# A fused transformer layer with 32 experts: slot 10 of the expert weights split into high and low words in single passes too

## The reference, cut to what matters

```python
logits = xt @ w_router + b_router            # 1024 tokens, 32 experts
top_vals, top_idx = lax.top_k(logits, 4)
gates = jax.nn.softmax(top_vals, axis=-1)
...
h = xblk @ w1[e] + b1[e]                     # w1[e] is 1024 x 2048
yb = clamped_swiglu(h) @ w2[e] + b2[e]       # w2[e] is 1024 x 1024
out = zeros.at[tok_buf].add(yb * gate_buf)   # added back by token
```

## Time and profile before

| | us |
|---|---|
| median of 3 runs | 2165.43 |
| lowest and highest | 2163.07 and 2165.44 |
| the profiled execution | 2162.8 |
| its span | 2161.1 |
| PE busy | 2080.2 (96%) |
| DVE busy | 1477.3 (68%) |
| ACT busy | 1192.9 (55%) |
| the loop of passes | 503.7 to 2147 |

### The profile page before, as it was taken

One profiled execution on the slowest core, in us unless ns is written; L12 is line 12 of the kernel. 1 busy time (PEld: TensorE's weight loads), 2 busy tenths in 40 slices (PEclk: granted clock), 3 DMA queues, 4 the chain that ended last, 5 costly groups with the idle time before them and its releaser, 6 DMA issues.

```text
span 2161.1 us, 35581 instructions
## 1 busy us (share of the span) xinstructions
PE 2080.2 (96%) x11530; PEld 1681.5 (78%) x11531; DVE 1477.3 (68%) x2291; ACT 1192.9 (55%) x1651; POOL 212.2 (10%) x201
## 2 busy tenths in 40 slices
PE   6999989988999999999999999999999999999997
PEld 4443678866799778877979797977779979888895
DVE  3251486668866787688676767678986666567666
ACT  3241375246645676567564646477764555555545
POOL 2000300012101111011010101011010110101001
PEclk9999999989999999999999999999999999999999
DMA  7000302118966699689686868679996677668556
GB/s 269 1 0 6 144 27 88 40 55 321 357 227 207 231 340 355 194 324 358 232 275 240 268 234 262 231 258 368 336 373 212 194 242 273 185 206 297 188 197 219
DMA packets 203128, 477.39 MB, mean 221 GB/s; under 512 B 14743, under 2 KB 20951, under 8 KB 203024
## 3 DMA queue, kind: packets, MB, share of 16 engines
q1 hardware_dynamic: 185598, 437.69, 55.9%
q0 software_dynamic: 17424, 39.17, 7.5%
q10 hardware_dynamic: 66, 0.02, 0.0%
HBM read 468.99 MB, written 32.11 MB: 232 GB/s over the span
## 4 chain that ended last, share of the span: by engine, by line
PE 71%; DVE 10%; issue 7%; DMA 6%; ACT 4%; DVEq 1%; ACTq 1%; POOLq 1%; SPq 0%; POOL 0%
PE ps L1288 16%; PE ps L1290 16%; PE ps L1289 16%; PE ps L1023 8%; DVE w_lo L1842 4%; DMA out<-y,idx_cur 4%; PE ps L1401 2%; DMA ring<-in_w 1%; PE ps L1168 1%; PE ps L1170 1%; PE ps L1169 1%; PE ps L1282 1%; ACT ring L719 1%; DMA xh<-in_x 1%; DVE xT L1842 1%
## 5 line engine op out<-in xcount | busy, mean ns | idle before, releaser
L890 ACT ACTIVATE w_hi<-ring 128x1024 fp32r<-128x1024 f32 x730 | 781.7, 1121 | 422.1 <-PE ps L1290 370.0
L1842 DVE TENSOR_TENSOR w_lo<-ring,w_hi 128x1024 fp32r<-128x1024 f32 x732 | 862.3, 1220 | 188.3 <-ACT w_hi L890 188.3
L1288 PE MATMUL ps<-xT,w_hi 128*128 128x256 f32 x1248 | 354.2, 284 | 0.0
L1290 PE MATMUL ps<-xT,w_lo 128*128 128x256 f32 x1248 | 353.1, 283 | 0.0
L1289 PE MATMUL ps<-xT,w_hi 128*128 128x256 f32 x1248 | 353.1, 283 | 0.0
L1288 PE MATMUL ps<-w_hi,xT 128*128 128x512 f32 x816 | 323.3, 396 | 13.2 <-issue 6.9
L1289 PE MATMUL ps<-w_lo,xT 128*128 128x512 f32 x816 | 319.5, 392 | 0.0
L1290 PE MATMUL ps<-w_hi,xT 128*128 128x512 f32 x816 | 319.5, 391 | 0.0
L1288 PE MATMUL ps<-w_hi,actT 128*128 128x512 f32 x644 | 262.8, 408 | 0.0
L1290 PE MATMUL ps<-w_hi,actT 128*128 128x512 f32 x644 | 251.6, 391 | 0.0
L1289 PE MATMUL ps<-w_lo,actT 128*128 128x512 f32 x644 | 251.1, 390 | 0.0
(11 more groups left out here) (312 smaller groups left out, 2400.7 us busy)
## 6 DMA issues: line engine op xcount, KB each, us to landing
ring<-in_w SPq DMA_DIRECT2D x390, 1024.0 KB, 7.2
xh<-in_x SPq DMA_DIRECT2D x4, 2048.0 KB, 16.1
work<-in_w_out SPq DMA_DIRECT2D x1, 4096.0 KB, 12.9
token_rows<-uT POOLq DMA_DIRECT2D x8, 512.0 KB, 2.9
out<-xh SPq DMA_DIRECT2D x8, 512.0 KB, 9.1
work<-in_w_in SPq DMA_DIRECT2D x2, 1536.0 KB, 18.0
uT<-in_w_mem_kv SPq DMA_DIRECT2D x1, 2048.0 KB, 14.5
ring<-in_w_in SPq DMA_DIRECT2D x1, 1536.0 KB, 16.9
```

The lines of the kernel that those rows point to most:

```text
L890: act_e.activation(hi, raw, ACT.Copy).then_inc(hi_ready, counted(h, whole))
L1288: pe.matmul(acc, hi, whi, start=first, stop=False, skip_group_check=shared)
L1290: return pe.matmul(acc, lo, whi, start=False, stop=last, skip_group_check=shared)
L1842: return dve.tensor_tensor(lo, x, hi.bitcast(F32), ALU.subtract)
```

## The change

The tuple of slots left whole becomes empty. In single passes ACT now copies the high words of slot 10 and DVE subtracts its low words and releases the raw buffer; ACT writes the high words of piece 2 to `actT_hi` and DVE subtracts the low ones, behind slot 11, at the place that the loop over j has for it; PE makes slot 10 out of the three products like the others. The waits follow by the same tuple: PE waits for the low words of piece 2 before it transposes piece 3 and before slot 10 (lines 1324 and 1385), DVE waits for PE's ordinary counts, and ACT waits with slot 14 for slot 10's use of the word ring (line 886).

```diff
--- before.py
+++ after.py
@@ -53,7 +53,7 @@
 SPLIT = 8
 LEAD = 6
 LEAD_POOL = 4
-WHOLE = (10,)
+WHOLE = ()
 AHEAD_OOB = 1 << 20
```

## The result

| | before | after |
|---|---|---|
| median | 2165.43 (2163.07 to 2168.44) | 2401.72 (2399.28 to 2404.17) |
| span of the profiled execution | 2161.1 | 2399.7 |
| PE busy | 2080.2 | 2115.2 |

The ratio is 1.109, with a 95% interval from 1.108 to 1.111. The change makes the kernel 236 us slower; 37 us were forecast. The sign was right and the size was wrong by a factor of six.

The account below looks back on a forecast made before the run. PE was taken as busy 96% of the span, with DVE and DMA close behind and DVE's order deciding. Terms of 17.6 + 12.8 + 5.9 + 0.7 + 0.65 = 37.6 us led to 2202 us predicted, range 2184 to 2213.

Parts of the forecast that it names:

- the loop's head: Start of DVE's loop, between passes: its overhead was carried over unchanged at 1.40 us.
- The rivals: Four other outcomes: 2152 us (chance 0.05), about 2165 (0.04), 2185 (0.09), 2210 to 2212 (0.14).
- PE's gain: Slot 10 on PE, split into 12 products: 0.70 us gained per single pass, 13.3 us in all.
- The low words of piece 2: DVE in single passes: 20.05 us from idx_next until PE turns piece 3, against 17.66, holding PE 2.4 us.
- The place is what costs: DVE in single passes: slot 10 subtracted early, piece 2's low words behind slot 11, PE held 2.4 us.
- not its sum: DVE in a steady single pass: the order of its work decides, its sum being 33.05 of 37.22 us.
- A single pass behind a double one: Nine passes: PE's turn of piece 3 comes 2.65 us later, less 0.70 gained: +1.95 us each, 17.6 us.
- A single pass behind a single one: Eight passes, a ring through result copy, scatter and DVE: +1.6 us each, between +1.1 and +2.4; 12.8 us.
- more is lost: Rival for steady single passes: scatter lands no sooner, +2.4 us each, 2210 to 2212 us in all; chance 0.14.
- A double pass behind a single one: Nine passes: PE's wait for group 1's tokens grows by 0.65 us each, 5.9 us in all.
- The first passes: First two passes together: PE, which started late, waits less for DVE and loses only 0.7 us.

Follow-up runs that it names:

- a32: The changed kernel with 32 tiny memsets put ahead of DVE's loop, the loop itself unchanged: 2213.8 us, ratio 1.022 to before.
- a32_order: a32 with DVE, in single passes only, subtracting the low words of piece 2 ahead of slot 11: 2201.7 us, ratio 1.017.
- a32_order_cut: a32_order with both DVE subtractions of slot 10 in single passes cut to one column: 2180.2 us, ratio 1.007.
- b4: The kernel before, unchanged but for 4 tiny memsets ahead of DVE's loop: 2506.0 us, ratio 1.157.

## Why the prediction was wrong

*The step that failed: the loop's head.* The prediction carries "the loop's overhead of 1.40 us" over from before, and treats each edit as costing its own work and its place in the order. The change makes DVE's loop four instructions longer, 266 to 270, and with that it reaches into a fourth piece. The idle time ahead of sel is about 6.5 us behind a double pass and 9.6 to 12.5 behind a single one, where it was 2 at the most. By the table that is 188 of the 236 us (after less a32). The rivals had none of this kind, so the range could not hold the time. A row of before spoke of it: sel waits on "issue" 39.0 us in total, which is time for the sequencer, and the page counts the packets of the instruction queue. Neither says how near the border is; the compiled program does. The page Runtime: NRT & Kernel Launch of the Trainium skill (Instruction fetch mechanics) says that a taken branch to a target outside the pages at hand stalls for a fetch. That rule belonged among the rivals. Its sizes don't fit what was seen here: it has blocks of 256 instructions and a window of two, while these runs have packets of 128 and fetch nothing for a loop over three of them.

*PE's gain: right.* From the turn of piece 3 to the next pass it is 6.42 us before and 5.72 in after and a32, 0.70 less as forecast.

*The low words of piece 2: right.* 20.06 us were measured in a32 from idx_next to the turn, by the sum 20.05, and the wait of 2.47 us stands where it was said to stand. But a32_order shows that this place was not what cost: with it mended the wait stood at slot 11 and, the clock apart, the time stayed. "The place is what costs" did not hold, nor that DVE's order decides and "not its sum": less work on DVE gave 21.5 us (a32_order_cut), another order only the clock back.

*A single pass behind a double one: mis-sized.* 1.95 us forecast, 3.0 measured (23.8 over 8). Without the 1.6 us of the clock in six of them it is 1.8. That the wait which the change brings could lower PE's clock stood in no term.

*A single pass behind a single one: mis-sized.* 1.6 us forecast between 1.1 and 2.4; measured 2.36, or 1.8 without the 1.6 us of the clock in three of the eight. The scatter lands no sooner in five of them (8.9 to 10.3 us, where the earlier trace rows has 8.9) and in 7.2 to 7.6 us in the other three, which take 37.4 to 37.5 us. So the rival "more is lost" was right in part, and that its 2210 to 2212 is nearly a32's time is luck: it had no clock in it. In after itself the second scatter of a double pass lands sooner (7.1 us where a32 has 8.1), of which 0.6 us is POOL's issue (1.6 us against 2.2), in whose first third DVE stands still there; the loads, stretched over longer passes, may do the rest. PE waits 0.3 to 1.1 us instead of 2.5 at the turn in all but one of these passes and keeps its clock, and a single pass behind a double one takes 39.0 us there and 41.4 in a32.

*A double pass behind a single one: too much.* 0.65 forecast, 0.1 measured. PE's wait for the tokens of group 1 did not grow: 2.6 us in 9 waits before, 1.7 in 5 in a32. Which step ahead of it came sooner I did not take apart.

*The first passes: too little.* 0.7 forecast, 4.2 measured, of which 2.7 in the first; I did not take it apart.

That a32 is within 12 us of the forecast is in part luck, then: terms too small by 8.2, 6.1 and 3.5 us stand against two that are too large by 5.0 and 1.4.

## What to carry to other kernels

A loop has a size in instructions on each engine, and a border that it may cross: compare idle time behind "issue" at the loop's first instruction, and the packets on the instruction queue, before and after any edit, and when both jump, move the code by a few instructions before judging the edit. A gap of an engine in a profile can be what another one lives on: POOL's scatter was cheap while DVE stood still beside most of it. In a ring where each engine is nearly full, moving one step within an engine moves the wait, and the price is known only from the whole ring.

## What was not expected of the hardware

- DVE's instructions are fetched in packets of 8192 bytes, 128 instructions. A loop over three such pieces fetched nothing from its second pass to its last; one over four fetched 5 packets in each pass, at 6 to 17 us of idle time ahead of the loop's first work.
- Four tiny writes far ahead of the loop made the kernel before 15.7% slower.
- POOL's issue of the same indirect DMA took 1.62, 2.75, 3.5 or 5.8 us, by the work that DVE had beside it; with a pause in that work it ended 1.5 us after DVE stopped.
- PE's products went from 0.23 to 0.42 us apart (granted clock 0.64 over 2.8 us) after a wait of 2.0 to 2.5 us in nine passes of a32, and not after one of 2.35 to 2.49 us in four others. What decides stays open.
- Not settled: why the stops are longer in b4 than in after, why a pass over four pieces fetches five packets, and which of DVE's instructions hold POOL's issue off most.
